# Second layer's input projection: five weight subtractions, the Hyena products and the folds on GpSimd instead of VectorE

## The reference

```
h  = modulate(rmsnorm(x))                       # for latent and for context tokens
proj = h @ w_in                                 # 1024 x 3856, columns K V XB DT | C Q Z HY
y_ssd = bidirectional Mamba-2 scan of XB, DT, C, gated by Z
y_att = GQA(QK-RMSNorm, 2-D rotary) of Q, K, V
u = dwconv3(HY);  v, x1, x0 = split(u)
y_hy  = x0 * long_conv(v * x1)                  # by a Fourier transform of length 512
x = x + g1 * (concat(y_ssd, y_att, y_hy) @ w_out)
x = x + g2 * swiglu(modulate(rmsnorm(x)))
```

## Time and profile before

| | |
|---|---|
| median of 3 runs | 1243.56 us |
| the profiled execution | 1244.54 us |
| its span | 1242.7 us |
| TensorE (PE) busy | 1202.8 us, 97% |
| VectorE (DVE) busy | 821.6 us, 66% |
| ScalarE (ACT) busy | 523.6 us, 42% |
| GpSimd (POOL) busy | 1.7 us |
| stage "in" of the second layer, TensorE | about 807 to 958 us |

### The profile page before, as it was taken

The page is one execution under the profiler, slowest core; times in us unless marked ns, Lnnn a source line. Parts: engine busy times, 40 slices in busy tenths (PEclk is TensorE's granted clock), DMA queues, the critical chain, the costliest instruction groups (busy, mean ns, idle before and its releaser), DMA issues. The chain is left out here.

```text
span 1242.7 us, 16729 instructions
## 1 busy us (share of the span) xinstructions
PE 1202.8 (97%) x6774; PEld 962.6 (77%) x6774; DVE 821.6 (66%) x1287; ACT 523.6 (42%) x907; POOL 1.7 (0%) x8
## 2 busy tenths in 40 slices
PE   5999999999999999999999999999998999999998
PEld 3666877777676788888887778778888778889888
DVE  4664357868766646767646656566589876776674
ACT  4362445442544433222222222357576454443454
POOL 0000000000000000000000000000000000000000
PEclk8999999999999999999999999999999999999999
DMA  9733242432011145554575454323344223655653
GB/s 336 247 123 105 93 162 86 157 99 65 18 35 40 63 138 201 195 194 166 192 230 172 168 178 169 94 62 95 114 119 119 69 52 119 187 185 187 187 177 128
DMA packets 132388, 171.82 MB, mean 138 GB/s; under 512 B 9268, under 2 KB 112342, under 8 KB 132312
## 3 DMA queue, kind: packets, MB, share of 16 engines
q1 hardware_dynamic: 131828, 170.58, 42.5%
q10 hardware_dynamic: 484, 0.18, 0.1%
HBM read 169.69 MB, written 1.05 MB: 137 GB/s over the span
## 5 line engine op out<-in xcount | busy, mean ns | idle before, releaser
L1812 DVE TENSOR_TENSOR w_lo<-w_raw,w_hi 128x1024 fp32r<-128x1024 f32 (+1 forms) x220 | 263.9, 1204 | 174.6 <-ACT w_hi L1439 172.6
L1439 ACT ACTIVATE w_hi<-w_raw 128x1024 fp32r<-128x1024 f32 (+1 forms) x220 | 228.3, 1042 | 332.0 <-DMA w_raw<-in_w_gu_dram 143.7
L700 PE MATMUL ps<-h_hi,w_hi 128*128 128x512 f32 (+1 forms) x576 | 218.7, 380 | 0.9 <-DVE w_lo L1812 0.6
L702 PE MATMUL ps<-h_hi,w_lo 128*128 128x512 f32 (+1 forms) x576 | 212.7, 369 | 0.0
L701 PE MATMUL ps<-h_lo,w_hi 128*128 128x512 f32 (+1 forms) x576 | 212.4, 369 | 0.0
L700 PE MATMUL ps<-f_hi,w_hi 128*128 128x512 f32 (+1 forms) x472 | 167.7, 355 | 4.2 <-DVE att_lo L2362 2.7
L702 PE MATMUL ps<-f_hi,w_lo 128*128 128x512 f32 (+1 forms) x472 | 162.5, 344 | 0.0
L700 PEld LDWEIGHTS ps<-h_hi,w_hi 128*128 128x128 f32 x576 | 108.5, 188 | 26.9 <-issue 8.8
L702 PEld LDWEIGHTS ps<-h_hi,w_lo 128*128 128x128 f32 x576 | 108.5, 188 | 18.8
L701 PEld LDWEIGHTS ps<-h_lo,w_hi 128*128 128x128 f32 x576 | 108.6, 189 | 17.4
L711 PE MATMUL ps<-h_hi,w_hi 128*128 128x512 f32 x320 | 113.2, 399 | 0.4 <-ACT gate L1744 0.4
(11 more groups left out here) (342 smaller groups left out, 1910.0 us busy)
## 6 DMA issues: line engine op xcount, KB each, us to landing
w_raw<-in_w_gu_dram SPq DMA_DIRECT2D x88, 512.0 KB, 3.5
w_raw<-in_w_in_dram SPq DMA_DIRECT2D x60, 512.0 KB, 3.7
w_raw<-in_w_down_dram SPq DMA_DIRECT2D x32, 512.0 KB, 3.5
m_even<-in_w_mod_dram SPq DMA_DIRECT2D x14, 1024.0 KB, 5.9
m_odd<-in_w_mod_dram SPq DMA_DIRECT2D x14, 1024.0 KB, 5.8
m_raw<-in_w_mod_dram SPq DMA_DIRECT2D x24, 512.0 KB, 5.3
m_first<-in_w_mod_dram SPq DMA_DIRECT2D x16, 512.0 KB, 10.5
w_raw<-in_w_out_dram SPq DMA_DIRECT2D x16, 512.0 KB, 3.4
```

Of the source, the lines that this page charges most:

```text
L700: mm(o, w_hi[:, i % RING, w], hi[:, 0:n], start=first and k == 0, stop=False)
L702: last = mm(o, w_lo[:, i % RING, w], hi[:, 0:n], start=False, stop=final and k == nk - 1)
L1439: A(w_hi[:, i % RING, w], w_raw[:, i % RING, w], ACT.Copy).then_inc(w_hi_done, 1)
L1812: TT(w_lo[:, i % RING, w], w_raw[:, i % RING, w], w_hi[:, i % RING, w].bitcast(F32), ALU.subtract).then_inc(w_lo_done, 1)
```

## The change

In the second layer, pieces 15, 18, 21, 24 and 27 of stage "in" are split by GpSimd, and the two products v * x1 and their folds are made by GpSimd. VectorE leaves them out. GpSimd's order is: 15, 18, 21, product and fold of blocks 0 and 1, 24, 27, product and fold of blocks 2 and 3. A fold is two instructions of 128x256 there and not four of 128x128. TensorE's waits for `w_lo` go through `low_ready`, which waits for VectorE's count less GpSimd's pieces, and for GpSimd's own count `w_lo_pool` where one of its pieces is among the last two. At step 29 VectorE waits for GpSimd's `hyv_ready`. The first layer is unchanged.

```diff
+POOL_SPLITS = (15, 18, 21, 24, 27)
+def pool_splits(i):
+    return sum(PLAN[1, "in"][0] + s < i for s in POOL_SPLITS)
...
         @block.gpsimd
...
+            def split_piece(s):
+                i = g0 + s
+                pool.wait_ge(w_hi_done, i + 1)
+                nc.gpsimd.tensor_tensor(w_lo[:, i % RING, :], w_raw[:, i % RING, :], w_hi[:, i % RING, :].bitcast(F32),
+                                        ALU.subtract).then_inc(w_lo_pool, 1)
+            def fold_product(v2, ch):
+                for q in (q0 + ch - 1, q0 + ch):
+                    pool.wait_ge(pair_free[q % 2], q // 2 + 1)
+                pool.wait_ge(S["y_head_done"], 2 * HEADS)
+                done[0] += 1
+                nc.gpsimd.tensor_tensor(hyv[:, v2:v2 + 2, 0:L], hyv[:, v2:v2 + 2, 0:L], x1t[:, :, 0:L], ALU.mult).then_inc(pool_done, 1)
+                pool.wait_ge(pool_done, done[0])
+                for part, op in zip(halves, (ALU.add, ALU.subtract)):
+                    ins = nc.gpsimd.tensor_tensor(part[:, v2:v2 + 2, 0, :], hyv[:, v2:v2 + 2, 0:P], hyv[:, v2:v2 + 2, L - 1:P - 1:-1], op)
+                ins.then_inc(S["hyv_ready"], 1)
+            for s in POOL_SPLITS[:3]:
+                split_piece(s)
+            fold_product(0, 10)
+            for s in POOL_SPLITS[3:]:
+                split_piece(s)
+            fold_product(2, 12)
...
         @block.tensor
+            def low_ready(i):
+                pe.wait_ge(w_lo_done, i + 1 - pool_splits(i + 1))
+                if pool_splits(i + 1) > pool_splits(i - 1):
+                    pe.wait_ge(w_lo_pool, pool_splits(i + 1))
-                            pe.wait_ge(w_lo_done, i + half + 1)
+                            low_ready(i + half)
...
             def split_w(i):
-                if i < PIECES:
+                if i < PIECES and i - PLAN[1, "in"][0] not in POOL_SPLITS:
...
-                            if kind == "hy" and idx in (2, 3):
+                            if l == 0 and kind == "hy" and idx in (2, 3):
...
-                    if s in S_FOLD:
+                    if l == 0 and s in S_FOLD:
...
                     if s == S_FEAT:
-                        p.own("hyv_ready")
+                        dve.wait_ge(S["hyv_ready"], 2 * (l + 1))
```

More of the change, by code:

```diff
@@ L346, in backbone @@
         w_hi_done, w_lo_done, w_used = sem("w_hi_done"), sem("w_lo_done"), sem("w_used")
+        w_lo_pool = sem("w_lo_pool")
         pair_free = [sem("pair_free0"), sem("pair_free1")]
@@ L354, in backbone @@
         late_full = sem("late_full")
-        wdt_full, wdt_hi_done, wdt_split = sem("wdt_full"), sem("wdt_hi_done"), sem("wdt_split")
+        wdt_full, wdt_split, pool_done = sem("wdt_full"), sem("wdt_split"), sem("pool_done")
         out_stored = sem("out_stored")
@@ L600, in _ @@
                     pool.wait_ge(S["dt_psum"], l)
-                nc.gpsimd.tensor_copy(wdt_hl[:, :, 0:16], wdts[l][:]).then_inc(wdt_hi_done, 1)
-                pool.wait_ge(wdt_hi_done, l + 1)
+                nc.gpsimd.tensor_copy(wdt_hl[:, :, 0:16], wdts[l][:]).then_inc(pool_done, 1)
+                pool.wait_ge(pool_done, l + 1)
                 nc.gpsimd.tensor_tensor(wdt_hl[:, :, 16:32], wdts[l][:], wdt_hl[:, :, 0:16].bitcast(F32), ALU.subtract).then_inc(wdt_split, 1)
+            done = [DEPTH]
+            g0, q0 = PLAN[1, "in"]
+            def split_piece(s):
[19 more added lines that the diff above has]
+            fold_product(2, 12)
         @block.tensor
@@ L763, in first_half @@
                     part(k, w_hi, h_hi, k == 0)
-                pe.wait_ge(w_lo_done, g + 2)
+                low_ready(g + 1)
                 for k in range(2):
@@ L792, in h_pair @@
                 for half in range(int(first), 2):
-                    pe.wait_ge(w_lo_done, g + 2 * half + 2)
+                    low_ready(g + 2 * half + 1)
                     for k in range(4):
@@ L1103, in _ @@
                             if u == 0:
-                                pe.wait_ge(w_lo_done, i + 2)
+                                low_ready(i + 1)
                                 pair_open(q)
@@ L1126, in part_half @@
                     if j == 0:
-                        pe.wait_ge(w_lo_done, g0 + i + 1)
+                        low_ready(g0 + i)
                     if i > 0:
@@ L1277, in _ @@
                     i = g0 + PARTS + ch
-                    pe.wait_ge(w_lo_done, i + 1)
+                    low_ready(i)
                     if ch >= 2:
```

## The result

The kernel with the change takes 1246.94 us (median of 8 runs, 1245.19 to 1249.02); the one before, run beside it, 1242.53 (8 runs, 1240.89 to 1244.09). The ratio is 1.0037, with a 95% interval of 1.0027 to 1.0047: slower by 4.6 us (3.4 to 5.8), where 2.9 us faster was forecast. That is near rival 1, which had 4 us slower (1247.6). The number lies inside the stated range of 1239.3 to 1247.6 only because that range was stretched to rival 1; the forecast's own range ended at 1242.5. The profiled execution after took 1245.64 us, its span is 1243.8.

A forecast was written before the change was run, and what follows sets the result against it. TensorE's waits for VectorE, 5.62 us in the stretch, were taken as the bound; rows moved up step by step brought the transposes of v 2.9 us earlier: 1243.56 - 2.9 = 1240.7 us, range 1239.3 to 1247.6 (own range 1239.5 to 1242.5).

The forecast's parts named there:

- rival 1: VectorE's two-SBUF-input instructions stand still while GpSimd reads SBUF: 10.6 us lost against 6.3 saved, 1247.6 us; chance 0.29.
- TensorE's ten additional waits at no cost: Semaphore waits at pieces around GpSimd's, costed at nothing; bound 0.05 us each, 0.5 in all.
- Step 1: Without split 21 VectorE's row starts 1.14 us earlier; by L2102 of step 21 the lead shrinks to 0.85.
- Step 2: First rotated heads ready 0.85 us earlier; TensorE, 0.55 earlier, doesn't wait for them.
- Step 3: Without the product, the state of step 22 is ready 1.46 us earlier; TensorE still waits 0.58.
- Step 4: Without split 24 the second heads are ready 2.60 us earlier; TensorE waits 0.48, could start piece 24 at 934.95.
- Step 5: GpSimd's split of 24, behind product and fold, ends at 935.9; TensorE waits about 1 us, wins 1.65 there.
- Step 6: After piece 24 VectorE has slack (2.6 us); ScalarE's 2.89 us wait and the 0.33 at piece 28 go.
- Step 7: Transposes of v start at about 956.0 instead of 958.97, 2.9 us earlier; 5 us of cover hide the second fold.
- I count nothing given back: Behind the stage the chain after the transposes of v moves as a whole, so none of the gain is lost.
- Rival 2: VectorE and GpSimd only stretch each other, gain 1 to 2 us, or GpSimd is slow, gain 1.1; 1242.2 us; chance 0.19.
- Rival 3: VectorE wasn't the bound: behind each removed wait another as late, nothing won, 1243.5 us; chance 0.06.

The follow-up runs named there:

- e_best: Kernel before, with splits 22, 26, 30 and half of 24 on GpSimd beside PSUM work, VectorE's part of 24 behind the rotated heads: 1239.12 us, ratio 0.9979.
- e_idle: Changed kernel with only splits 15 and 18 on GpSimd, everything else back on VectorE: 1242.11 us, ratio 1.0005.
- e_order: Changed kernel with GpSimd's split of piece 24 put ahead of its first product and fold: 1244.79 us, ratio 1.0027.
- e_placed30: Kernel before, with splits 22, 26 and 30 on GpSimd, each gated to lie beside VectorE's PSUM work: 1240.38 us, ratio 0.9989.
- e_reorder: Kernel before, no GpSimd work added, VectorE's split of piece 24 moved behind the rotated heads: 1241.78 us, ratio 0.9999.
- e_pair: Kernel's computation left out; three VectorE instructions beside one of GpSimd: tensor_tensor from SBUF 2.15 us alone, 4.25 beside GpSimd's tensor_tensor.
- e_split: Changed kernel with only the five splits on GpSimd, products and folds back on VectorE: 1247.34 us, ratio 1.0050.

## Why the prediction was wrong

The failing assumption stands at the head of the sum: "I move the rows up", with VectorE's durations unchanged beside GpSimd's. The prediction named the opposite as rival 1, with the right mechanism and nearly the right price, and gave it 0.29 though it wrote itself "Against it no row speaks". A chance of 0.29 was too little for a mechanism with a stated rule for it (the Trainium skill, SBUF — State Buffer, Who interferes with whom) and no row on the other side; it should have been the forecast.

- **What bounds the kernel** (TensorE's waits for VectorE in this stretch): right. e_best took back 2.1 us of these waits and shortened the stage by 2.5.
- **What is removed**: 8.5 us on VectorE, of which splits 15 and 18 are worth nothing: right (e_idle). 6.3 us in the stretch: right as a count of instructions.
- **Sizes on GpSimd**: near. A split 2.36 to 2.40 us undisturbed (2.84 estimated; the 2.25 worked out from the figure of the Trainium skill, GPSIMD Engine Reference, 3.1 Elementwise, was nearer), a half fold 0.74 (0.80), a product 1.59 and 2.15 beside VectorE (1.48). No undisturbed product was seen, but the half split of e_best has its size, 128x512 with two inputs, and took 1.29.
- **TensorE's ten additional waits at no cost**: right (e_idle, two of the five splits). No row stood behind the bound of 0.05 us each.
- **Step 1** (VectorE's row 1.14 earlier): failed at once. GpSimd's split of 21 came up when its rounding was done, beside VectorE's split of 20, and stopped it for 2.19 us; TensorE had a new wait of 1.73 for `em`.
- **Step 2** (no wait for the first heads): true, but only since TensorE was itself late.
- **Step 3** (0.58 of wait for the state): 0.76, near, for the same reason.
- **Step 4** (second heads 2.60 earlier, 0.48 of wait): the step that carries the miss. 2.79 later against the mark, 4.07 of wait. The rotary products were stopped for 3.6 us by the product, the folds and the split of 24 behind them.
- **Step 5** (a new wait of 1 us for GpSimd's split of 24): didn't show. The split ended at 934.77, and TensorE stood for the heads until 936.60.
- **Step 6** (slack later, ScalarE's wait and the 0.33 at piece 28 gone): right.
- **Step 7** (transposes of v 2.9 us earlier): 3.55 later. The cover of the second fold held: it ended at 951.91, VectorE came to it at 957.73.
- **"I count nothing given back"** behind the stage: 0.5 us more there in the two profiles, not explained.
- **The clock**: no term of the sum, and named only as something that would make the working wrong. It was about 1.2 to 1.4 of the 3.55 us. Such a share is found by difference, stage less waits. Where the clock is full in the whole stage this difference against before should be zero. It is 0.0 in e_idle, but -0.2 in e_order, -0.4 in e_placed30 and in e_best and +0.6 in e_reorder, so each share is good to about half a us.

**Rival 1** put 10.6 us of standing still against 6.3 saved. Up to the second heads it was 5.78 against 2.89; the place (rotary instructions) and the price (+4) were right, though a third of the price came from the clock, which the rival didn't contain, so its number is partly luck. **Rival 2** (stretching, not blocking) is excluded by e_pair: of 2.26 us of overlap 2.10 were lost. **Rival 3** had no case: TensorE did win where VectorE was relieved without disturbance.

## What to carry to other kernels

Before giving GpSimd elementwise work, list what VectorE executes at those moments: beside instructions with two SBUF inputs, or fast single-input ones, the time of a GpSimd instruction that reads SBUF is VectorE's time, and 2.4 us of GpSimd for 1.14 us of VectorE is a loss; beside instructions that read one input from PSUM, and reductions, it cost VectorE nothing here (2.14 and 2.13 us either way). GpSimd starts when its semaphore comes up, not when it is needed, so gate it on the event ahead of the PSUM work. And count a long wait of TensorE for more than its length: the longest here (3.05, 3.70, 4.07 and 4.71 us) were each followed by half clock, and splitting one into two of 1.9 us saved 1.4 us at the same sum of waits.

## What the runs showed that I had not expected

A tensor_scalar with a single SBUF input loses as much as a tensor_tensor with two: 3.45 against 1.36 us beside GpSimd's tensor_tensor, and it loses 0.69 us beside a memset of 0.95, which leaves the two-input forms alone. The clock's fall isn't ruled by the length of a wait by itself: of the waits of 1.73 us for `em`, the one of e_split was followed by 0.51 from 916 to 918 (and its wait of 1.75 by 0.50 from 948 to 950), those of the change and of e_order by none. What else decides stays open.
